# Ring slots and left-operand tiles begin at different places within 512 bytes, and one product is issued in two halves

## The reference, cut to what matters

```python
proj = rmsnorm(x) @ w_in                       # 2048 x 8192
x = x + mixed @ w_out                          # 2048 x 2048
g, u = split(rmsnorm(x) @ w_gate_up)           # 2048 x 11264
x = x + (silu(g) * u) @ w_down                 # 5632 x 2048
# second block
proj = h @ w_in_2                              # 2048 x 8256
q = (rms(c_q) @ w_uq); kv = (rms(c_kv) @ w_ukv) # 512 x 1536, 512 x 2048
merged = sigmoid(gl_a) * (y_a @ w_proj_mla) + sigmoid(gl_b) * (y_b @ w_proj_sb)
x = x + gt1 * (merged @ w_out_2)               # 2048 x 2048
gate, up = split(h2 @ w_ffn_in_2)              # 2048 x 11264
x = x + gt2 * ((silu(gate) * up) @ w_ffn_out_2) # 5632 x 2048
```

## Time and profile before

| | |
|---|---|
| runs | 2608.65 and 2609.42 us, median 2609.03 |
| profiled execution, span from its first to its last instruction | 2606.9 us |
| TensorE busy | 2587.1 us, 99% of the span |
| VectorE busy | 1825.4 us, 70% |
| ScalarE busy | 1414.8 us, 54% |
| moved by DMA | 582.20 MB, mean 223 GB/s |

### The profile page before, as it was taken

One profiled execution on the slowest core, in us unless ns is written; L12 is line 12 of the kernel. 1 busy time (PEld: TensorE's weight loads), 2 busy tenths in 40 slices (PEclk: granted clock), 3 DMA queues, 4 the chain that ended last, 5 costly groups with the idle time before them and its releaser, 6 DMA issues.

```text
span 2606.9 us, 33516 instructions
## 1 busy us (share of the span) xinstructions
PE 2587.1 (99%) x11881; PEld 2145.5 (82%) x11881; DVE 1825.4 (70%) x2168; ACT 1414.8 (54%) x1861; POOL 14.6 (1%) x28
## 2 busy tenths in 40 slices
PE   9999999999999999999999999999999999999999
PEld 7888888878888888888788888888788888888887
DVE  5888888777777878888875545566687654445565
ACT  6555545465656465445566556544465556565443
POOL 1000000000000000000000000000000000000000
PEclk9999999999999999999999999999999999999999
DMA  7765556778888888887665555555578765655554
GB/s 247 253 194 178 170 151 205 268 262 291 283 292 285 291 285 297 283 293 253 199 202 157 167 171 160 184 204 186 183 269 289 254 198 191 195 190 197 192 193 172
DMA packets 302590, 582.20 MB, mean 223 GB/s; under 512 B 20133, under 2 KB 20913, under 8 KB 302097
## 3 DMA queue, kind: packets, MB, share of 16 engines
q1 hardware_dynamic: 301008, 576.26, 66.7%
q0 software_dynamic: 1008, 3.55, 0.4%
q10 hardware_dynamic: 464, 0.93, 0.1%
HBM read 578.55 MB, written 2.11 MB: 223 GB/s over the span
## 4 chain that ended last, share of the span: by engine, by line
PE 95%; DVE 3%; ACT 1%; issue 1%; DMA 0%; ACTq 0%; DVEq 0%
PE acc L328 30%; PE acc L330 30%; PE acc L329 30%; DVE lo L315 1%; PE aux L1131 1%; DVE op_lo L509 0%; PE tp L482 0%; DVE op_hi L508 0%; ACT stage L494 0%; PE tp L1105 0%; PE aux L2258 0%; PE aux L2257 0%; PE tp L542 0%; DMA rows<-attn_norm_w 0%; PE tp L1151 0%
## 5 line engine op out<-in xcount | busy, mean ns | idle before, releaser
L315 DVE TENSOR_TENSOR lo<-raw,hi 128x1024 fp32r<-128x1024 f32 x895 | 1077.2, 1222 | 430.5 <-ACT hi L309 409.6
L309 ACT ACTIVATE hi<-raw 128x1024 fp32r<-128x1024 f32 x895 | 928.3, 1056 | 528.5 <-PE acc L330 368.8
L328 PE MATMUL acc<-hi,op_hi 128*128 128x512 f32 x2752 | 1084.9, 394 | 8.5 <-DVE lo L315 5.9
L330 PE MATMUL acc<-hi,op_lo 128*128 128x512 f32 x2752 | 1072.1, 390 | 0.0
L329 PE MATMUL acc<-lo,op_hi 128*128 128x512 f32 x2752 | 1071.5, 389 | 0.0
L328 PEld LDWEIGHTS acc<-hi,op_hi 128*128 128x128 f32 x2752 | 516.9, 188 | 119.6 <-issue 11.2
L330 PEld LDWEIGHTS acc<-hi,op_lo 128*128 128x128 f32 x2752 | 516.6, 188 | 109.0
L329 PEld LDWEIGHTS acc<-lo,op_hi 128*128 128x128 f32 x2752 | 517.2, 188 | 102.6
L591 DVE SCALAR_TENSOR_TENSOR ada_acc<-ada_ring,cact,ada_acc 128x512 f32<-128x512 f32 x360 | 269.5, 749 | 7.6 <-DVE small L431 0.6
L328 PE MATMUL acc<-hi,f_hi 128*128 128x512 f32 x704 | 274.5, 390 | 0.1
L329 PE MATMUL acc<-lo,f_hi 128*128 128x512 f32 x704 | 273.9, 389 | 0.0
(11 more groups left out here) (336 smaller groups left out, 1284.0 us busy)
## 6 DMA issues: line engine op xcount, KB each, us to landing
raw<-w_in SPq DMA_DIRECT2D x257, 512.0 KB, 3.9
ada_ring<-w_ada SPq DMA_DIRECT2D x192, 512.0 KB, 5.3
raw<-w_gate_up SPq DMA_DIRECT2D x176, 512.0 KB, 5.2
raw<-w_ffn_in SPq DMA_DIRECT2D x176, 512.0 KB, 4.4
raw<-w_down SPq DMA_DIRECT2D x88, 512.0 KB, 5.8
raw<-w_ffn_out SPq DMA_DIRECT2D x88, 512.0 KB, 4.3
raw<-w_out SPq DMA_DIRECT2D x64, 512.0 KB, 4.1
raw<-w_proj_mla SPq DMA_DIRECT2D x16, 512.0 KB, 3.9
```

Source lines behind the costliest of these rows:

```text
L309: A.activation(hi[:, k, :, 0:n], raw[:, k, :, 0:n], ACT.Copy).then_inc(hi_ready, 1)
L315: V.tensor_tensor(lo[:, k, :, 0:n], raw[:, k, :, 0:n], hi[:, k, :, 0:n].bitcast(F32), ALU.subtract).then_inc(lo_ready, 1)
L328: T.matmul(dst, lh, hi[:, k, kk, 0:n], start=first and kk == 0, stop=False)
L330: mm = T.matmul(dst, ll, hi[:, k, kk, 0:n], start=False, stop=last and kk == CK - 1)
```

## The change

Three edits. The four slots of `hi` no longer begin at multiples of 4096 bytes but 0, 16, 48 and 112 elements further (0, 64, 192 and 448 bytes), those of `lo` 0, 8, 32 and 96 elements further (0, 32, 128 and 384 bytes); each ring has 512 bytes more, so that what lies behind keeps its place within 512 bytes. The tiles of `op_hi` are 272 elements apart instead of 256, so that tile `kt` begins at 64 x `kt` bytes within 512; `op_lo`, `raw`, `f_hi`, `f_lo`, `lat_hi`, `lat_lo`, `ya_hi` and `ya_lo` stay as they were. In the stage `up` the product of line 328 is issued as two matmuls of 256 columns, each with a load of the same left tile.

```diff
--- before.py
+++ after.py
@@ -30,6 +30,10 @@
 NB = 512
 CK = 2
 RING = 4
+HI_STARTS = (0, 16, 48, 112)
+LO_STARTS = (0, 8, 32, 96)
+SLOT_ROOM = 128
+TILE_ROOM = 16
 ADA_RING = 2
 EPS = 1e-6
 DH = 1024
@@ -115,9 +119,13 @@
 
         ada = sb("ada", [P, ADA * 4])
         raw = sb("raw", [P, RING, CK, NB])
-        hi = sb("hi", [P, RING, CK, NB], F32R)
-        lo = sb("lo", [P, RING, CK, NB], F32R)
-        op_hi = sb("op_hi", [P, KT, S], F32R)
+        hi, lo = [], []
+        for ring, name, starts in ((hi, "hi", HI_STARTS), (lo, "lo", LO_STARTS)):
+            whole = sb(name, [P, RING * CK * NB + SLOT_ROOM], F32R)
+            for k in range(RING):
+                first = k * CK * NB + starts[k]
+                ring.append(whole[:, first:first + CK * NB].rearrange("p (a n) -> p a n", n=NB))
+        op_hi = sb("op_hi", [P, KT, S + TILE_ROOM], F32R)[:, :, 0:S]
         op_lo = sb("op_lo", [P, KT, S], F32R)
 
 
@@ -306,16 +314,16 @@
             act.wait_ge(raw_ready[k], i * (per // RING * 16) + 16 * (c // RING) + 16)
             if c >= RING or later(i):
                 act.wait_ge(chunk_used, i * per + c - RING + 1)
-            A.activation(hi[:, k, :, 0:n], raw[:, k, :, 0:n], ACT.Copy).then_inc(hi_ready, 1)
+            A.activation(hi[k][:, :, 0:n], raw[:, k, :, 0:n], ACT.Copy).then_inc(hi_ready, 1)
 
         def dve_chunk(dve, c, i, per, n=NB):
 
             k = c % RING
             dve.wait_ge(hi_ready, i * per + c + 1)
-            V.tensor_tensor(lo[:, k, :, 0:n], raw[:, k, :, 0:n], hi[:, k, :, 0:n].bitcast(F32),
+            V.tensor_tensor(lo[k][:, :, 0:n], raw[:, k, :, 0:n], hi[k][:, :, 0:n].bitcast(F32),
                             ALU.subtract).then_inc(lo_ready, 1)
 
-        def pe_chunk(pe, c, i, per, into, kt, first, last, n=NB, left=(op_hi, op_lo), half=None, late=None):
+        def pe_chunk(pe, c, i, per, into, kt, first, last, n=NB, left=(op_hi, op_lo), half=None, late=None, halves=False):
 
             k = c % RING
             pe.wait_ge(lo_ready, i * per + c + 1)
@@ -325,9 +333,13 @@
                         pe.wait_ge(op_ready, late)
                     lh, ll = (o[:, kt + kk, t * P:(t + 1) * P] for o in left)
                     dst = into[:, t, 0:n]
-                    T.matmul(dst, lh, hi[:, k, kk, 0:n], start=first and kk == 0, stop=False)
-                    T.matmul(dst, lh, lo[:, k, kk, 0:n], start=False, stop=False)
-                    mm = T.matmul(dst, ll, hi[:, k, kk, 0:n], start=False, stop=last and kk == CK - 1)
+                    if halves:
+                        for c0 in (0, n // 2):
+                            T.matmul(dst[:, c0:c0 + n // 2], lh, hi[k][:, kk, c0:c0 + n // 2], start=first and kk == 0 and c0 == 0, stop=False)
+                    else:
+                        T.matmul(dst, lh, hi[k][:, kk, 0:n], start=first and kk == 0, stop=False)
+                    T.matmul(dst, lh, lo[k][:, kk, 0:n], start=False, stop=False)
+                    mm = T.matmul(dst, ll, hi[k][:, kk, 0:n], start=False, stop=last and kk == CK - 1)
                 if t == 0 and half is not None:
                     mm.then_inc(half, 1)
             mm.then_inc(chunk_used, 1)
@@ -1723,7 +1735,7 @@
 
         def all_tiles(ring, c):
 
-            return ring[:, c % RING].rearrange("p a (b n) -> p (a b) n", n=ROPE)
+            return ring[c % RING].rearrange("p a (b n) -> p (a b) n", n=ROPE)
 
         C2 = CH["in2"]
         G_UP, G_SB, G_GATE, G_PP, G_OUT, G_END = (CH[n] - C2 for n in ("up", "in2b", "in2c", "pp", "out2", "gu2"))
@@ -1776,7 +1788,7 @@
                 c = C2 + G
                 if G == 16:
                     sp.wait_ge(lo_ready, c - RING + 1)
-                    sp.dma_start(all_tiles(raw, c), a["w_in_2"][0].rearrange("(k p) n -> p k n", p=P)[:, :, C_PE:C_SB]).then_inc(raw_ready[c % RING], 16)
+                    sp.dma_start(raw[:, c % RING].rearrange("p a (b n) -> p (a b) n", n=ROPE), a["w_in_2"][0].rearrange("(k p) n -> p k n", p=P)[:, :, C_PE:C_SB]).then_inc(raw_ready[c % RING], 16)
                 elif G < G_UP or G_SB <= G < G_PP:
                     sp_chunk(sp, c, 0, 4, in2_src(G))
                 elif G < G_SB:
@@ -2345,7 +2357,7 @@
                     k = (G - G_UP) % 2
                     kt = CK * k + (0 if G - G_UP < 6 else 4)
                     pe.wait_ge(lt["split"], kt // 2 + 1)
-                    pe_chunk(pe, c, 0, 4, into, kt, k == 0, k == 1, left=(lat_hi, lat_lo))
+                    pe_chunk(pe, c, 0, 4, into, kt, k == 0, k == 1, left=(lat_hi, lat_lo), halves=True)
                 elif G < G_PP:
                     k = (G - (G_SB if G < G_GATE else G_GATE)) % 8
                     pe_chunk(pe, c, 0, 4, into, CK * k, k == 0, k == 7)
```

## The result

The changed kernel takes 2651.05 us (median of 2650.81 and 2651.28) against 2609.03 before: a ratio of 1.0161, 95% interval 1.0132 to 1.0191. It is 42 us slower. I had forecast no effect, 2609.5; the result lies 3 us above the upper end of the range.

A forecast was written before the change was run, and what follows sets the result against it. TensorE's matmul stream was taken to bound the kernel: 2606.9 us span + 0 (slots) + 0 (op_hi tiles) + 0.3 (halves) = 2607.2, with 2.1 around it 2609.3, written as 2609.5. Range 2580 to 2648; likeliest case 2604 to 2615.

The forecast's parts named there:

- What bounds the kernel: Whole kernel: TensorE's stream of matmuls, busy 2587.1 of 2606.9 us, sets the time; each matmul takes 226.5 ns.
- The count of 10,740: Whole kernel: 895 chunks of 12 matmuls, at 226.5 ns each 2432.6 us, 93% of the span.
- the slots of hi and lo: TensorE's moving tiles: three slots in four begin off the 512-byte grid, 8055 matmuls; claimed 0 us.
- The ends around the term: Slots' possible cost over all 10,740 matmuls: plus 4.6 ns each (+49 us) to minus 12.0 ns each (-129 us).
- 0 against 256: Key product: loads begin at 0 and 256 bytes in turn, yet 256-column matmuls keep 113.3 ns; read as no effect.
- The lone matmul: Line 330 at 542.04 us, no load beside it: 388 ns against 389; read as loss belonging to the moving stream.
- The streams never settle: Rival, changing starts keep matmuls at the unsettled pace: 4.6 ns each, 2634 if half are hit, 2659 if all; chance 0.20.
- nine matmuls behind a small one: From 104.00 to 106.08 us, behind small matmuls: 231.1 ns each before settling, all addresses the same as when settled.
- A crossing of each 512-byte line: Rival: each 512-byte block touched costs 3.3 ns; 8055 off-grid tiles touch five, +27 us, 2636; chance 0.10.
- Equal starts are what costs: Rival: load and stream starting alike cause the loss; other starts save 12.0 ns each, up to 129 us, 2480; chance 0.15.
- The tiles of op_hi: Loads beginning at 64 x kt bytes stay hidden behind matmuls: 0 us; VectorE's writes there 0, at most 1 us.
- The halves: Stage `up`: 56 matmuls become 112 of 256 columns at 113.3 ns; claimed +0.3 us, between -0.7 and +4.9.

## Why the prediction was wrong

*What bounds the kernel* was right: TensorE's pace and nothing else. The span grew by 42.5 us and its busy time by 43.0. The count of 10,740 should have been 10,728, since the key product's chunk has other matmuls.

*The step that failed* is the one for the slots of hi and lo: "I take 0: a moving stream reads one tile from front to back wherever it begins, and the one pair of starts that the trace has besides equal ones, 0 against 256, costs nothing." The slots alone cost 27 us. The ends around the term were sound, from -129 to +49 us, and the truth for slots and tiles together, +42, was near the upper one. The value was taken from a single pair, and the runs show that this pair is the exception: the cost repeats each 256 bytes as far as was tried, so 0 and 256 are the same place. The other half of the reason, that a stream is read alike wherever it begins, is true only while the loaded tiles move with it. A row that shows no effect at one distance is no evidence for the distances between. Had I asked which of the change's places covers, the answer was hardly any: the slots and tiles move by 32 to 448 bytes, and of all moved places only two of the 16 tiles of op_hi begin at 256.

*The lone matmul* was read too widely. I took from it that the 13.3 ns of the old kernel don't come from the next load, and no run speaks against that: a shorter load loses none of them, and 2-byte parts lose 10.8. But I used it against any contest of load and stream, and the starts of loads and streams against each other are what the change pays for. The same place in the run with both rings at 64 bytes, a matmul with no load beside it, in groups:

```profile
L342 PE MATMUL acc<-hi,op_lo 128*128 128x512 f32 x1 | 0.4, 397 | 0.0
L341 PE MATMUL acc<-lo,op_hi 128*128 128x512 f32 x1 | 0.4, 392 | 0.0
```

397 instead of 388 ns, still without a load at its side. The trace has nine such matmuls: eight last 397 ns and the last one, on `f_lo`, 388. Before, all nine last 388. So the extra seems not to be two reads at the same instant either; the ends of matmuls are modelled, so this isn't shown.

*The rivals.* "The streams never settle" named the right price: 231.1 ns from nine matmuls behind a small one, 231.1 measured in `gu2`, and 2659 us if all matmuls are hit, with 2651 measured. It had 0.20. That the two 231.1 agree is in part chance, since the four slots of `gu2` lie between 229.4 and 233.3 ns. Its reason was half right: a change of distance costs about three matmuls each time, but a constant wrong distance costs as well, up to 7.5 ns. "A crossing of each 512-byte line" had its sign come true, 229 to 231 ns in three slots of four of `dn2`, and is false all the same: it fell with the run that shifts everything. "Equal starts are what costs" was the opposite of the truth: starts that are equal within 256 bytes are the only free ones of those tried.

*The tiles of op_hi* were costed at 0 as loads that stay hidden. A load's record still lasts 188 ns and fits under the matmul, but its address counts: alone the tiles cost 33 us, so this 0 failed like the one for the slots. That their cost is "not a second sum" beside the slots' was right as to the ends: 27 and 33 us alone, 42 together, still below +49.

*The halves* were right in that they hardly matter: +0.3 us forecast, 0.5 us between medians measured, inside the noise, and 0.9 us in the stretch itself. The working was too good: the halves follow at 116 and not 113.3 ns, and the two products behind them pay 6 and 7 ns, a cost for which the forecast had no term.

*The rule on the ports.* The rule of the Trainium skill, SBUF — State Buffer, "Who interferes with whom", that TensorE's two read ports are independent and that TensorE never waits on anyone spoke for no effect. The measurement decides: 64 bytes between the two cost 21 or 65 us here, depending on the side. Whether the ports are the reason, no run tells.

What stays open is the mechanism. Shown is that the cost depends on the starts of moving and loaded tiles against each other, modulo 256 bytes, on the order of distances, on the load's length, on where a product is cut in halves, and on the width of the elements (of both operands at once). Why 64 bytes one way cost 2.2 ns and the other way 6.7, and why a matmul without a load beside it has the longer record, no run tells.

## What to carry to other kernels

Where float32r matmuls of 512 columns run back to back, let every moving tile and every loaded tile begin at the same place within 256 bytes, and pad rows and slots by multiples of that; whether all lie on the grid or all 64 bytes off it made no difference. When a trace is to show that an address doesn't matter, check first that it holds the distances in question and not one that is equivalent to zero. If the accuracy allows it, 2-byte parts save 10.8 of the 13.3 ns and, at the four places tried, the sensitivity too.

## What the runs showed of the hardware that I had not expected

A settled float32r matmul of 512 columns takes 226.67 ns at the clock's upper level, 17/16 of the 213.3 ns that 512 ticks last, steady over 1810 matmuls; with bfloat16 it is 215.8. Of the distances between moving and loaded tile, only 0 and 256 bytes gave that pace; all others tried cost 2.2 to 7.5 ns. Two products of 512 columns behind a product in two halves took 233 ns each at distances that are free otherwise. Loading 64 or 32 columns instead of 128 raised the pace from 226.67 to 230.0 and 231.7 ns. Bfloat16 loads last 98 ns by their records instead of 188.
